# mLSTM decay rows issued from ScalarE's queue instead of GpSimd's, in a hybrid attention and mLSTM block

## What is computed

```python
lf = jax.nn.log_sigmoid(fg)
...
bcum = jnp.cumsum(fc, axis=-1)
D = jnp.where(causal, bcum[..., :, None] - bcum[..., None, :] + ic[..., None, :], -jnp.inf)
inter = bcum + m[..., None]
m_t = jnp.maximum(inter, jnp.max(D, axis=-1))
s = jnp.einsum('bhtd,bhsd->bhts', qc, kc) * jnp.exp(D - m_t[..., None])
num = w_inter[..., None] * jnp.einsum('bhvd,bhtd->bhtv', C, qc) + jnp.einsum('bhts,bhsv->bhtv', s, vc)
h = num / jnp.maximum(jnp.abs(nq), jnp.exp(-m_t))[..., None]
```

## Time and profile before

| what | value |
|---|---|
| median of three runs | 318.14 us |
| the profiled execution, its own time | 318.38 us |
| its span, first to last instruction | 316.6 us |
| TensorE matmul busy | 308.4 us, 97% |
| VectorE busy | 225.9 us, 71% |
| ScalarE busy | 164.9 us, 52% |
| GpSimd busy | 96.7 us, 31% |
| `decay_rows`, issues on GpSimd | 16, 9.0 us |
| DMA moved | 38.30 MB; 34.51 by SyncE's queue, 3.34 by GpSimd's, 0.14 by ScalarE's |
| granted TensorE clock | 0.996 |

### The profile page before, as it was taken

The page is one execution under the profiler, slowest core; times in us unless marked ns, Lnnn a source line. Parts: engine busy times, 40 slices in busy tenths (PEclk is TensorE's granted clock), DMA queues, the critical chain, the costliest instruction groups (busy, mean ns, idle before and its releaser), DMA issues.

```text
span 316.6 us, 4991 instructions
## 1 busy us (share of the span) xinstructions
PE 308.4 (97%) x1595; PEld 255.7 (81%) x1595; DVE 225.9 (71%) x509; ACT 164.9 (52%) x337; POOL 96.7 (31%) x121
## 2 busy tenths in 40 slices
PE   7999999999999999999999999999999999999992
PEld 4888888878888888888888888778888888888882
DVE  3544999748998699968998568965577766856534
ACT  3448856287345324573147573385556976453201
POOL 3701006066450114002220026592711984000000
PEclk9999999999999999999999999999999999999998
DMA  7941553956725486654865433211220474310111
GB/s 233 313 99 36 158 144 94 164 154 155 142 69 135 135 151 204 182 144 114 181 193 183 114 77 88 71 66 34 67 68 0 127 185 157 134 68 0 66 68 67
DMA packets 29177, 38.30 MB, mean 121 GB/s; under 512 B 3672, under 2 KB 15296, under 8 KB 29152
## 3 DMA queue, kind: packets, MB, share of 16 engines
q1 hardware_dynamic: 27424, 34.51, 36.7%
q0 software_dynamic: 1568, 3.34, 7.3%
q10 hardware_dynamic: 160, 0.14, 0.1%
HBM read 33.68 MB, written 4.29 MB: 120 GB/s over the span
## 4 chain that ended last, share of the span: by engine, by line
PE 82%; DVE 7%; issue 4%; DMA 3%; ACT 2%; DVEq 0%; POOLq 0%; POOL 0%; SPq 0%; ACTq 0%
PE bank L1501 21%; PE bank L1503 21%; PE bank L1502 20%; PE bank L1553 4%; PE bank L1849 3%; PE bank L1793 3%; DMA w_raw<-in_w_in 3%; PE bank L1814 3%; PE bank L1646 2%; DVE w_lo L1061 2%; DVE farena L1173 1%; PE bank L1743 1%; PE bank L1534 1%; PE bank L1804 1%; PE bank L1647 1%
## 5 line engine op out<-in xcount | busy, mean ns | idle before, releaser
L788 ACT ACTIVATE w_hi<-w_raw 128x512 fp32r<-128x512 f32 x71 | 43.7, 626 | 63.1 <-PE bank L1503 50.8
L1501 PE MATMUL bank<-w_hi,xT_hi 128*128 128x512 f32 (+1 forms) x180 | 72.5, 403 | 0.0
L1503 PE MATMUL bank<-w_hi,xT_lo 128*128 128x512 f32 (+1 forms) x180 | 69.7, 387 | 0.0
L1502 PE MATMUL bank<-w_lo,xT_hi 128*128 128x512 f32 (+1 forms) x180 | 69.4, 385 | 0.0
L1061 DVE TENSOR_TENSOR w_lo<-w_raw,w_hi 128x512 fp32r<-128x512 f32 x64 | 45.6, 724 | 10.3 <-ACT w_hi L788 10.2
L1501 PE MATMUL bank<-xT_hi,w_hi 128*128 128x512 f32 x128 | 50.8, 397 | 0.0
L1503 PE MATMUL bank<-xT_hi,w_lo 128*128 128x512 f32 x128 | 50.1, 392 | 0.0
L1502 PE MATMUL bank<-xT_lo,w_hi 128*128 128x512 f32 x128 | 50.0, 390 | 0.0
L1503 PEld LDWEIGHTS bank<-w_hi,xT_lo 128*128 128x128 f32 x180 | 33.8, 188 | 7.1
L1501 PEld LDWEIGHTS bank<-w_hi,xT_hi 128*128 128x128 f32 x180 | 33.9, 188 | 5.9 <-issue 0.4
L1502 PEld LDWEIGHTS bank<-w_lo,xT_hi 128*128 128x128 f32 x180 | 34.0, 189 | 5.5
(11 more groups left out here) (215 smaller groups left out, 583.4 us busy)
## 6 DMA issues: line engine op xcount, KB each, us to landing
w_raw<-in_w_in SPq DMA_DIRECT2D x72, 256.0 KB, 3.0
w_raw<-in_w_out SPq DMA_DIRECT2D x16, 256.0 KB, 2.9
kq_rows<-stage SPq DMA_DIRECT2D x8, 256.0 KB
gy<-kq_rows SPq DMA_DIRECT2D x8, 256.0 KB, 3.5
gy<-in_x SPq DMA_DIRECT2D x4, 512.0 KB, 5.9
out_y<-gy SPq DMA_DIRECT2D x7, 256.0 KB, 2.0
farena<-in_x SPq DMA_DIRECT2D x4, 256.0 KB, 4.3
farena<-in_x SPq DMA_DIRECT2D x2, 512.0 KB, 6.3
```

The costliest lines, as they stand in the source:

```text
L788: a.activation(hi, raw, ACT.Copy).then_inc(w_hi_done, 1)
L1501: pe.matmul(o, hi, m_hi, start=start, stop=False)
L1502: pe.matmul(o, hi, m_lo, start=False, stop=False)
L1503: return pe.matmul(o, lo, m_hi, start=False, stop=stop)
```

## The change

`decay_rows` moves from GpSimd's list to ScalarE's. For head 0 it stands at slot 14, behind `cut(20)`, and waits for `g_out`. For head h + 1 it stands behind the last `pm_high` of head h, with the same wait for `pm_done` as before. The DMAs, their order, sizes and semaphore are the same. GpSimd no longer waits for `g_out`; its masks still wait for `g_back`.

```diff
             g.dma_start(g_dram, rows[4]).then_inc(g_out, 16)
-            g.wait_ge(g_out, 16)
-
-            def decay_rows(h):
-
-                if h:
-                    g.wait_ge(pm_done, NT * h)
-                for j in range(NT):
-                    g.dma_start(decay[j], g_dram[4 * j + h:4 * j + h + 1, j * P:].to_broadcast([P, SEQ - j * P]))\
-                        .then_inc(g_back, 16)
...
-            decay_rows(0)
             decay_mask(0)
...
             for h in range(1, MH):
-                decay_rows(h)
                 head_rsqrt(2 * h - 2)
...
+            def decay_rows(h):
+
+                if h:
+                    a.wait_ge(pm_done, NT * h)
+                else:
+                    a.wait_ge(g_out, 16)
+                for j in range(NT):
+                    a.dma_start(decay[j], g_dram[4 * j + h:4 * j + h + 1, j * P:].to_broadcast([P, SEQ - j * P]))\
+                        .then_inc(g_back, 16)
...
+                if b == S_QK + 6:
+                    decay_rows(0)
...
                     if b - 2 in PE_ST and PE_ST[b - 2][0] == h:
                         pm_high(*PE_ST[b - 2])
+                        if PE_ST[b - 2][1] == NT - 1 and h < MH - 1:
+                            decay_rows(h + 1)
```

## The result

The median of 22 runs is 319.70 us for the changed kernel and 317.95 us for the kernel before. The ratio is 1.0069, with an interval of 1.0046 to 1.0092; ratios here come from all the runs of both kernels, not from the two medians, whose quotient is 1.0055. The forecast was 317.3 us in a range of 316.7 to 318.8, so the time lies outside the range, and the sign is the other one. The profiled execution took 318.89 us for a span of 317.1, at a granted clock of 0.996. With 318.38 us before, the two profiled executions differ by 0.5 us, where the medians differ by 1.75.

What follows compares the result with a forecast made beforehand. The prediction took the kernel as one stream of TensorE matmuls, busy 97% of the span. Closing head 0's hole gave -0.84 us, heads 1 to 3 gave 0: 318.38 to 317.5 us profiled, 317.3 us as median, range 316.7 to 318.8.

Steps and rivals of the forecast that it cites:

- the place: TensorE's hole before head 0's second score product, 69.17 to 70.24 us: 0.84 us to gain; heads 1 to 3: 0.
- The point at which the hole closes: Slot 24's load must land 0.84 us earlier, at 64.14 us at the latest, everything behind it keeping its length.
- What a closed hole is worth: Closing head 0's hole at 69 us was to save 0.84 us and give 317.3 us, with chance 0.62.
- the price of an issue: Each of head 0's four issues on ScalarE costs 0.50 us: 2.0 us in all, range 1.3 to 4.1, delaying nothing.
- its moment: ScalarE issues head 0's rows between the cuts of slots 20 and 21, from about 55.1 us.
- the length of the burst: Head 0's four decay transfers, 3.7 to 10.7 us considered; low half taken, last landing about 61 to 63 us.
- the sign of a wrong forecast: Head 0's burst still taking 8 us or more, or the hole at 69 us moved or grown.
- rival A: Head 0's burst is slow because of the row it reads; hole stays within some tenths, 318.1 us; chance 0.25.
- the -0.84 us of the sum: Head 0's term: the hole before its second score product closes fully; the only nonzero term.
- who is caught in the burst: Loads of slots 22 and 23 run ahead of it, some 3 us each; slot 24 lands in 3.0 to 4.0.
- rival B: Slot 24's load falls deep in the burst, takes 9.8 us, chain slides 4.1 us: 322.2 us; chance 0.07 beyond 0.5%.
- The rule against the change: Transfers use the same 16 engines whoever issues them; another issuer saves only issuing time, so the burst's cost stays.

Runs made afterwards that it cites:

- the four holes with GpSimd's early issue: Kernel before (0.84 us), its unchanged repeat (0.64), it with only heads 1 to 3 on ScalarE (0.39), it with eight memsets ahead of the issues (0.37).
- head 0 alone: Against the kernel before, only head 0's decay rows issued by ScalarE, heads 1 to 3 still by GpSimd: 319.46 us, ratio 1.0056.
- the two profiles above: Kernel before with GpSimd issuing head 0's rows behind the first silu (321.17 us, ratio 1.0094), and the unchanged changed kernel profiled again (323.05 us).
- the changed kernel's second: Changed kernel run and profiled again without any edit: median 319.44 us, ratio 1.0060; the profiled execution took 323.05 us.
- the later issue: Changed kernel with head 0's rows issued by ScalarE behind the second convolution's silu: 323.95 us, ratio 1.0174.

## Why the prediction was wrong, point by point

**Right: the place.** The edit acts at one place, the hole in front of the second score product of head 0, through the load of slot 24. Heads 1 to 3 cost nothing on TensorE: 124.00 of 124.00 us, as the earlier trace rows said. The point at which the hole closes was right too: slot 24 landing at 64.14, which is 59.28 + 4.86, the same 4.86 us as in the table. What a closed hole is worth is not refuted: where an earlier issue closes it, the median is 317.14 us (by its ratio 317.6), and the forecast for a closed hole was 317.3; but the interval of that ratio, 0.9965 to 1.0016, holds no gain at all as well.

**Right: the price of an issue, wrong: its moment.** The four issues took 0.84 + 1.39 = 2.23 us, 0.56 each, for an estimate of 0.50. The cut behind them stood 1.29 us for them, and the silu still began at 57.60, when VectorE let it: nothing was lost, as forecast. But I placed them "from about 55.1 us", behind the end of the cut of slot 20. They began at 53.62, while the previous instruction still ran (53.52 to 54.16) and ahead of the start of the cut, at 54.06, that stands in front of them in ScalarE's list. So in this trace ScalarE's DMA issues did not wait for the start of the instruction ahead of them. I had the burst 1.2 us behind slot 22's load, and it came 0.17 behind it; how the hole would look at 1.2 no run shows.

**The step that failed: the length of the burst.** I had 3.7 us from `gains` below, 10.7 us above and 8.4 us from head 2 between them, and took the low half. Measured: 11.0 us, above the upper end, and over the 8 us that I had named as the sign of a wrong forecast. `gains` reads a row too, but an input's, and one transfer of 256 KB alone; the decay rows were four transfers from rows that had just been written, beside weight loads. With 16 copies of the source the burst takes 6.1 to 6.8 us on either queue, which is rival A's reason. Even that is above `gains`. The nearest row was head 2's own burst: the same tiles, the same source, only another time. An analogue with the same source should have weighed more than one with the same kind of queue. The term that fell with it is the -0.84 us of the sum: in its place the hole grew by 0.94. But the length alone does not decide: issued one slot early the burst took 9.0 us and left no hole. What decides is how much of it lies beside slot 24's load.

**Its consequence: who is caught in the burst.** I wrote that the loads of slots 22 and 23 would be "now ahead of the burst" and take some 3 us each. Slots 22 and 23 did come earlier, and ScalarE's wait for slot 23 fell from 4.02 to 1.73 us; but then it waited 3.68 us for slot 24. The shared time went from one load to the next, which is the one on the chain. I had it landing in 3.0 to 4.0 us, and it took 6.64. That was rival B's mechanism, in small: it named 9.8 us for slot 24, and 66.6 us as the landing from which it decides. The load landed at 65.44, under that point, so in the profiled execution B is 0.94 us of hole and no more. I gave it 0.07, and 0.10 to all ways of being slower by over 0.5%, which is where the ratio came out, because I took slot 24 for safe 4 us behind the burst's start.

**Rival A** had the right reason and the wrong sum. It let the burst only shift and left the hole "within some tenths". The hole grew to 1.8 to 2.2 us: A took slots 22 and 23 for landed early and slot 24 for caught as before, 5.7 us, where it was 6.64 to 7.08.

**Missing altogether: the clock behind the hole.** Two things lie between the 0.5 us of the profiles and the 1.75 us of the medians. The profile before had the longest hole of its kind and a longer first wait. The mean of the four holes with GpSimd's early issue is 0.56 us, that of 1.78 and 1.89 (the changed kernel and head 0 alone) 1.84, which is 1.28 more; the 12 short runs of the changed kernel have a median of 319.23 us, 1.28 above 317.95. And the 10 other runs of the changed kernel are 1 to 4 us longer than those, most at a lower mean clock; they lift the median by the remaining 0.47 us. The sum had no term for what TensorE does after it has stood still. In the two profiles above it is about 1.7 us, nearly as much as the hole itself. A hole's price was taken as its length, and that holds only for the short ones of the kernel before.

**The rule against the change.** The Trainium skill, "DMA: Bandwidth & Descriptors", section "Issuing engines are not separate DMA queues", speaks against the change, and the runs agree with it: the burst took 11.0 us by ScalarE's queue against 10.7 us by GpSimd's, and 10.9 us by GpSimd's once it issues behind the same silu.

**What stays open.** Why a burst that starts 0.8 to 1.4 us later against the loads of slots 22 and 23 still leaves slot 24's load 0.9 to 1.9 us longer was seen and not explained: how the DMA engines share their time between the queues was not looked at. Why one source row is slow is open too; the runs show only that copies cure it. The upper group at a normal clock (such as 7 of 12 runs with heads 1 to 3 by ScalarE) is open, and so is the slow stretch in the first 10 us of two profiled executions (the changed kernel's second, and the later issue's), where the granted clock reads 1.00.

## What to carry to other kernels

A transfer moved to another engine's list is moved in time, too, and that is what to cost: write down which loads are issued within a microsecond of its old and its new moment, and which of them stands on the chain. Price its length by the same transfer elsewhere in the kernel, from the same source, and not by a transfer that merely uses the new queue. When a rate is set by what is read, ask for copies or an earlier place before another queue (and count what they cost: the copies here brought no time that could be measured), and do not price a hole in TensorE's stream at its length alone without a row that shows the clock behind it.

## What the hardware showed that I had not expected

- A broadcast of one row of DRAM, just written, to 128 partitions is slow: 640 KB in 9.0 to 11.7 us beside weight loads and 8.4 us with little beside it, against 6.1 and 6.8 us for the same bytes from 16 copies. At head 2's place, with the same packets, one row took 2.4 to 2.5 times the DMA engines' time.
- ScalarE's queue issued two DMAs from 53.62 on, while the engine was still in the instruction that began at 53.52, and before the cut at 54.06 that precedes them in the list.
- Holes of 2.03, 2.22 and 3.99 us in TensorE's stream were followed by a granted clock of about half for some 3 to 4 us; those of 0.37 to 1.89 us in the other profiles were not.
- A delay of 0.8 to 1.4 us can cost as much as itself and more: first issues 0.16 to 0.61 us behind slot 22's load in place of 0.68 to 0.83 ahead of it took the hole from 0.4 to 0.8 us up to 1.8 to 2.2.
